# One more seven-product pair in each of five feed-forward stages that also sum modulation vectors, and an earlier split ahead of the gates

## The reference

```python
def swiglu(h, w_gu, w_down):                       # width 1024 -> 2 x 2816 -> 1024
    gate, up = jnp.split(h @ w_gu, 2, axis=-1)
    return (jax.nn.silu(gate) * up) @ w_down

for i in range(DEPTH):                             # 4 layers
    x = x + 0.5 * swiglu(rmsnorm(x, ffn1_norm[i]), ffn1_w_gu[i], ffn1_w_down[i])
    x = x + mixer_i(rmsnorm(x, mix_norm[i]))       # gated delta net, stick-breaking, sparse attention, gated delta net
    x = x + 0.5 * swiglu(rmsnorm(x, ffn2_norm[i]), ffn2_w_gu[i], ffn2_w_down[i])

m = jnp.split((jax.nn.silu(c) @ mod_w[i] + mod_b[i])[:, None, :], N_MOD, axis=-1)      # 9 vectors of 1024 for each of 2 layers
mc = jnp.split(jax.nn.silu(c_ctx) @ mod_w[i] + mod_b[i], N_MOD, axis=-1)               # of these only the first 5 of layer 0
```

## Time and profile before

| | us |
|---|---|
| median of 3 runs | 3553.44 |
| profiled execution | 3552.46 |
| its span | 3550.7 |
| PE busy | 3453.6 (97%) |
| DVE busy | 2463.1 (69%) |
| ACT busy | 1846.2 (52%) |
| POOL busy | 145.2 (4%) |

### The profile page before, as it was taken

How to read it: one execution, slowest core, us unless ns; L and a number is a source line. 1 busy time by engine, 2 the same in 40 slices (tenths; PEclk the granted TensorE clock), 3 DMA queues, 4 the chain that set the end, 5 groups by cost and what they waited for, 6 DMA issues and landing times. The chain is left out here.

```text
span 3550.7 us, 45283 instructions
## 1 busy us (share of the span) xinstructions
PE 3453.6 (97%) x18348; PEld 2924.5 (82%) x18348; DVE 2463.1 (69%) x2749; ACT 1846.2 (52%) x2151; POOL 145.2 (4%) x152
## 2 busy tenths in 40 slices
PE   9999999999999998999999999999999999999999
PEld 7889888888888888788889878787889678788877
DVE  5776657666666678566677668787866567786586
ACT  5454354544645445545454456666654455655464
POOL 0001100000000000000001100000000000000000
PEclk9999999999999999999999999999999999999999
DMA  6642156664467663576752157575744247574574
GB/s 265 239 154 84 60 190 237 220 235 172 157 255 266 255 243 119 202 276 247 272 189 101 67 185 259 201 249 197 245 151 166 72 154 249 196 249 140 189 233 161
DMA packets 95741, 692.40 MB, mean 195 GB/s; under 512 B 10672, under 2 KB 10800, under 8 KB 12208
## 3 DMA queue, kind: packets, MB, share of 16 engines
q1 hardware_dynamic: 79344, 574.15, 43.0%
q0 software_dynamic: 16192, 115.35, 11.5%
HBM read 650.66 MB, written 1.05 MB: 184 GB/s over the span
## 5 line engine op out<-in xcount | busy, mean ns | idle before, releaser
L2392 DVE TENSOR_TENSOR w_lo<-raw,w_hi 128x2048 fp32r<-128x2048 f32 x468 | 1067.6, 2289 | 330.7 <-ACT w_hi L1662 330.5
L1662 ACT ACTIVATE w_hi<-raw 128x2048 fp32r<-128x2048 f32 (+1 forms) x470 | 895.5, 1909 | 372.5 <-PE acc L702 259.5
L700 PE MATMUL wrk<-w_hi,h_hi 128*128 128x512 f32 (+1 forms) x2040 | 796.1, 390 | 13.8 <-issue 5.4
L702 PE MATMUL wrk<-w_hi,h_lo 128*128 128x512 f32 (+1 forms) x2040 | 784.2, 384 | 0.0
L701 PE MATMUL wrk<-w_lo,h_hi 128*128 128x512 f32 (+1 forms) x2040 | 783.0, 384 | 0.0
L700 PEld LDWEIGHTS wrk<-w_hi,h_hi 128*128 128x128 f32 x2040 | 384.3, 188 | 94.5 <-issue 15.8
L700 PE MATMUL acc<-w_hi,hid_hi 128*128 128x512 f32 (+1 forms) x1160 | 453.5, 391 | 4.2 <-DVE hid_lo L2494 3.7
L702 PE MATMUL acc<-w_hi,hid_lo 128*128 128x512 f32 (+1 forms) x1160 | 450.1, 388 | 0.0
L701 PE MATMUL acc<-w_lo,hid_hi 128*128 128x512 f32 (+1 forms) x1160 | 449.7, 388 | 0.0
L702 PEld LDWEIGHTS wrk<-w_hi,h_lo 128*128 128x128 f32 x2040 | 383.9, 188 | 77.0
L701 PEld LDWEIGHTS wrk<-w_lo,h_hi 128*128 128x128 f32 x2040 | 384.6, 189 | 71.2 <-issue 0.2
(11 more groups left out here) (326 smaller groups left out, 4969.2 us busy)
## 6 DMA issues: line engine op xcount, KB each, us to landing
raw<-in_wts SPq DMA_DIRECT2D x469, 1024.0 KB, 4.9
arena<-in_mods POOLq DMA_DIRECT2D x72, 1024.0 KB, 5.1
arena<-in_wts SPq DMA_DIRECT2D x72, 1024.0 KB, 7.7
arena<-arena POOLq DMA_DIRECT2D x36, 1024.0 KB, 7.5
const<-in_const SPq DMA_DIRECT2D x1, 2112.0 KB, 17.3
c<-in_bias POOLq DMA_DIRECT2D x8, 256.0 KB, 2.9
x<-in_x SPq DMA_DIRECT2D x2, 512.0 KB, 6.7
c<-in_c SPq DMA_DIRECT2D x1, 1024.0 KB, 4.9
```

Of the source, the lines that this page charges most:

```text
L700: nc.tensor.matmul(o, l_h, r_h, start=first, stop=False, skip_group_check=True)
L702: return nc.tensor.matmul(o, l_l, r_h, start=False, stop=last, skip_group_check=True)
L1662: return nc.scalar.activation(o, i, f, **kw)
L2392: tt(w_lo[:, ns % SLOTS, :], v, w_hi[:, ns % SLOTS, :].bitcast(F32), ALU.subtract).then_inc(lo_ready, 1)
```

## The change

1. Five stages of the first block (`ffn1_1`, `ffn2_1`, `ffn1_2`, `ffn2_2`, `ffn1_3`), all with modulation, get one pair at step 5. `ffn1_0` and `ffn2_0` stay without.
2. The modulation jobs are single operations of 128 x 1024 on chunks of 512 KB (before: two operations on 1 MB). Their buffers leave the arena: `m_raw` is now `h_tok` (two chunks), `m_prod` is `row`; the last operation on a chunk writes its product over the chunk itself. POOL starts the loads of a stage when the norm's statistics are done (they use `h_tok`), and ACT waits at the start of every feed-forward stage for the jobs before it.
3. In a stage with a pair `mod_plan` shares the jobs over the ten units by `room`: none in unit 0 and in the pair, 3 in unit 1, 2 in the one ahead of the pair, 4 in each other. Up to four are set singly: behind `hid_low`, behind `gated`, and behind each of the two splits that follow. For 26 jobs this gives 0, 2, 4, 3, 2, 0, 4, 3, 4, 4, for the 28 jobs of `ffn1_1` 0, 2, 4, 4, 2, 0, 4, 4, 4, 4. POOL's T3 and T4 additions stand between its chunk loads.
4. In `ffn_pairs` of all stages, a unit that follows a single step splits the piece behind d (the next g(s+1,0), or the first block B11) ahead of the silus (ACT) and ahead of the `gated` operations (DVE). And the sum T2 of a stage's first pair is no longer preceded by the split of B21.

```diff
-PAIRS = {n: (2, 5, 8) for n in ("ffn2_3", "b0_ctx", "b0_ffn0", "b0_ffn1", "b1_ffn0", "b1_ffn1")}
+PAIRS = {n: (5,) for n in ("ffn1_1", "ffn2_1", "ffn1_2", "ffn2_2", "ffn1_3")}
+PAIRS |= {n: (2, 5, 8) for n in ("ffn2_3", "b0_ctx", "b0_ffn0", "b0_ffn1", "b1_ffn0", "b1_ffn1")}
...
-MOD_JOBS = [(m, w) for m in range(MOD_PIECES) for w in range(2 if 2 * m < CTX_CHUNKS else 1)]
+MOD_JOBS = [(k, w) for k in range(2 * MOD_PIECES) for w in range(2 if k < CTX_CHUNKS else 1)]
...
+def mod_plan(name):
+
+    plan, jobs = units(name), mod_jobs(name) if name in MOD_OPS else []
+    pair = [kind == "pair" for kind, _ in plan] + [False]
+    room = [0 if k == 0 or pair[k] else 2 if pair[k + 1] else 3 if k == 1 else 4 for k in range(len(plan))]
+    ends = [len(jobs) * sum(room[:k + 1]) // sum(room) for k in range(len(plan))]
+    return [jobs[a:b] for a, b in zip([0] + ends, ends)]
...
-        m_raw, m_prod = area(3072, 2, PW), area(3072 + 2 * PW, 2, PW)
+        m_raw, m_prod = h_tok, row
... (ScalarE, ffn_pairs)
-                    split_to(at("d", owed[-1]))
+                    split_to(at("d", owed[-1]) + (len(owed) == 1))
... (ScalarE, main loop)
-                if kind in ("gdn", "sb", "dsa") and mods_before(i):
+                if kind in ("gdn", "sb", "dsa", "ffn") and mods_before(i):
... (VectorE, modulation)
-                m, w = MOD_JOBS[g]
-                l = 2 * m // (9 * KC)
-                dve.wait_ge(mod_landed[m % 2], 16 * (m // 2 + 1))
-                if g:
+                k, w = MOD_JOBS[g]
+                l = k // (9 * KC)
+                dve.wait_ge(mod_landed[k % 2], 16 * (k // 2 + 1))
+                v, last = m_raw[:, k % 2, :], g + 1 == len(MOD_JOBS) or MOD_JOBS[g + 1][0] != k
+                if not last and g > 1:
+                    dve.wait_ge(mod_sums, g - 1)
+                elif last and w:
                     dve.wait_ge(mod_sums, g)
-                for b in range(2):
-                    j = 2 * m + b - l * 9 * KC
-                    ins = stt(m_prod[:, b, 0:D], m_raw[:, m % 2, b * D:(b + 1) * D], 1.0, m_rows[:, w, :], ALU.mult, ALU.mult, accum_out=der[:, l, w, j:j + 1])
+                j = k - l * 9 * KC
+                ins = stt(v if last else m_prod[:], v, 1.0, m_rows[:, w, :], ALU.mult, ALU.mult, accum_out=der[:, l, w, j:j + 1])
                 ins.then_inc(mod_sums, 1)
... (VectorE, ffn: of a step's jobs two, not one, stand behind hid_low)
-                    for g in mine[:1]:
+                    for g in mine[:2]:
... (VectorE, ffn_pairs)
                     if ahead is not None:
                         add_blocks("T1", ahead)
+                    mine = jobs[k]
+                    for g in mine[:1]:
+                        modulation(g)
...
-                    split_to(at("d", owed[-1]))
+                    split_to(at("d", owed[-1]) + (len(owed) == 1))
                     gated(s, 0)
                     gated(s, 1)
+                    for g in mine[1:2]:
+                        modulation(g)
                     split_to(at("d", owed[-1]) + 1)
+                    for g in mine[2:3]:
+                        modulation(g)
                     if ahead is not None:
-                        if ahead == PAIRS[name][0]:
-                            split_to(at("d", owed[-1]) + 2)
                         add_blocks("T2", ahead)
                     if s < STEPS - 1:
                         split_to(at("d", owed[-1]) + 2)
+                    for g in mine[3:]:
+                        modulation(g)
                 hid_low(STEPS - 1)
... (GpSimd, modulation)
-                if before(i, "x"):
-                    pool.wait_ge(x_new, before(i, "x"))
+                pool.wait_ge(rstd_ready, 2 * before(i, "norm") + 2)
...
+                for n, mine in enumerate(jobs):
+                    if n + 1 < len(plan) and plan[n + 1][0] == "pair":
+                        block_sum(i, plan[n + 1][1], "T3")
+                    if plan and plan[n][0] == "pair":
+                        block_sum(i, plan[n][1], "T4")
+                    for g in mine:
+                        k, w = MOD_JOBS[g]
+                        if k + 2 < end and (g + 1 == len(MOD_JOBS) or MOD_JOBS[g + 1][0] != k):
+                            pool.wait_ge(mod_sums, g + 1)
+                            load(k + 2)
```

More of the change, by code:

```diff
@@ L125 @@
 CTX_CHUNKS = 5 * KC
[L127 removed]
+MOD_JOBS = [(k, w) for k in range(2 * MOD_PIECES) for w in range(2 if k < CTX_CHUNKS else 1)]
 def mod_jobs(name):
     a = mod_start(name)
[L133 removed]
+    return [g for g, (k, _) in enumerate(MOD_JOBS) if a <= k // 2 < a + MOD_SHARE[name]]
+def mod_plan(name):
[4 more added lines that the diff above has]
+    return [jobs[a:b] for a, b in zip([0] + ends, ends)]
 ARENA = 15104
@@ L2513, in ffn @@
                         split_to(ns + 3 * s + 3)
-                    for g in mine[1:]:
+                    for g in mine[2:]:
                         modulation(g)
@@ L2627, in ffn_pairs @@
                     dve.wait_ge(rstd_ready, 2 * before(i, "norm") + 2)
+                jobs = mod_plan(name)
                 factors()
@@ L3393, in gdn, with block_sum @@
                                                 ALU.mult).then_inc(stage("gdn_lts"), 1)
+            def block_sum(i, s, which):
+                g = starts[i]["pairs"] + PAIRS[ops[i][1]].index(s)
+                if which == "T3":
+                    pool.wait_ge(block_landed[HOME["B22"]], 16 * (g + 1))
+                    pool.wait_ge(sum_ready, 2 * g + 1)
+                else:
+                    pool.wait_ge(lo_ready, ring_at[i, ("B21", s)] + 1)
+                    pool.wait_ge(sum_ready, 2 * g + 2)
+                pool.dma_start(blocks[HOME[which]], blocks[HOME[ADDED[which]]], accum_op=ALU.add).then_inc(added[which], 16)
@@ L3395, in modulation @@
             def modulation(i, name):
-                start = mod_start(name)
                 if name in ROWS_IN:
                     pool.wait_ge(taken, use[name, "mrow3"] + 1)
-                if before(i, "x"):
-                    pool.wait_ge(x_new, before(i, "x"))
[L3403 to L3413, removed]
+                pool.wait_ge(rstd_ready, 2 * before(i, "norm") + 2)
+                end = 2 * (mod_start(name) + MOD_SHARE[name])
+                def load(k):
+                    v = mods_d[k // 2]
+                    pool.dma_start(m_raw[:, k % 2, :], v[:, k % 2 * D:(k % 2 + 1) * D]).then_inc(mod_landed[k % 2], 16)
@@ new lines, in modulation @@
+                load(2 * mod_start(name))
+                load(2 * mod_start(name) + 1)
+                plan = units(name) if name in PAIRS else []
+                jobs = mod_plan(name) if plan else [mod_jobs(name)]
+                for n, mine in enumerate(jobs):
[8 more added lines that the diff above has]
+                            load(k + 2)
@@ L3433, in attn @@
                         load(n + 1)
[L3435 to L3448, removed]
             pool.wait_ge(ident_loaded, 16)
@@ L3460, in _ @@
                     modulation(i, name)
-                if name in PAIRS:
-                    block_sums(i, name)
+                elif name in PAIRS:
+                    for s in PAIRS[name]:
+                        block_sum(i, s, "T3")
+                        block_sum(i, s, "T4")
 def chunks(v):
```

## The result

The changed kernel takes 3562.74 us (median of 13 runs, 3556.97 to 3574.64) against 3553.78 us of the kernel before (13 runs, 3549.52 to 3556.31); the ratio is 1.0027, interval 1.0019 to 1.0035. It is slower by 9 us, forecast were 3.5 us less. Its profiled execution took 3559.18 us (span 3557.3), 6.7 more than that of before.

A forecast was written before the change was run, and what follows sets the result against it. It took PE, busy for 97% of the span, as the bound. Terms -17.7 - 11.5 + 5.5 + 15.1 + 5.1 = -3.5 us against 3552.46 us gave 3549 us, own range 3543 to 3556.

The forecast's parts named there:

- Part 1: Six stages that already had pairs: the new order removes the first pair's gap and its clock drops, -17.7 us.
- Rival (d): First pairs of the old pair stages: reordering does nothing, since B21 takes T2's place; +17.7, 3567 us; chance 0.06.
- Part 2: Five new pairs: -11.5 us from fewer matmuls, +5.5 us from their openings, entries at nothing.
- Rival (b): Entry to the new pairs is late behind two jobs; up to 18 us, 3558 to 3567 us; chance 0.13.
- Part 3: Last step of the five stages: jobs and a late chunk, landing in 3.7 us, delay `hid_low(10)`; +15.1 us.
- Part 4: Clock at the new gaps in the five stages: 3.9 drops of 1.3 us, +5.1 us.
- at 5.1 us 5.6 more: Last step, bound over four stages: if a 512 KB load lands in 5.1 us, 5.6 us more loss.
- (a): Last step: the last chunk isn't late enough to matter; 3539 us, or 3543 with two drops; chance 0.27.
- (c): Last step: the last chunk lands as late as the slowest load, 8.2 us; +18, 3567 us; chance 0.06.

The follow-up runs named there:

- the order alone: The kernel before with only the earlier split and the sum T2 ahead of B21's split in the six old pair stages; 3535.5 us, ratio 0.9951.
- low_first: The changed kernel with hid_low(10) ahead of the third and fourth modulation job in the last unit; 3550.75 us, ratio 0.9995.
- last_one: The changed kernel with one modulation job instead of four in the last unit of the five stages (two in `ffn1_1`); 3541.03 us, ratio 0.9966.
- no_new_pairs: The changed kernel without its five new pairs, keeping 512 KB chunks, their buffers and the new order; 3535.0 us, ratio 0.9951.

## Why the prediction was wrong

**Part 1, right.** Forecast -17.7, measured -18.7 in the changed kernel and in the order alone. The gap is gone in all six stages, no drop follows, and `ffn2_3` is 184.4 us where 184.6 was forecast. Rival (d) is out.

**Part 2, nearly right.** Pairs and openings by themselves bring -5.8, forecast was -6.0. The five openings lose 1.1 us each, as forecast. The entries were put at nothing, with 0.1 us of room; they lose 1.0, 0.8 and 1.0 us in three of the four stages with one job on a chunk, 2.9 us in all. Rival (b) looked for this at the second job of the entry and set it aside, since "that chunk is asked for some 10 us ahead". For that job this holds: it was 11.0 us in `ffn2_1`, and the load took 8.6. The wait is at the last job of the unit before, whose chunk is asked for 4.4 us ahead of its turn and takes 9.4 us (in `ffn1_2` and `ffn1_3` 9.5 and 9.4; in `ffn2_2` the same job waits 4.2 us and PE loses nothing). The units with several jobs were priced by the jobs' own durations, 13.0 us of 16.8, without any wait for a chunk; with the wait `hid_low` starts 2.0 us behind the transposes (1023.92 to 1025.93) and not 1.26, more than the 0.1 us of room.

**Part 3, the step that failed.** "I take 3.7" us for the landing of 512 KB. The last loads of the four stages took 5.1 to 5.6 us, and the ones before them 4.9 to 8.0. PE's end gaps are 2.4, 3.8, 6.6, 4.3 and 6.5 us (start to start less 0.227), 23.7 together, against 18.0 forecast in part 4: 5.7 us more. The bound "at 5.1 us 5.6 more" is just that. The mechanism was right, each gap ends on `hid_lo` behind chunk waits, and `ffn1_1` came out near the 2.2 us of the forecast. Wrong was to price a half-size load by its size, between a 256 KB load and 1 MB loads: the median landing was 5.5 us against 5.1 for the whole piece. Sorted by what the program had in flight at the issue, the 144 loads say more. Seven had nothing beside them and took 4.0 to 4.4 us, still more than 3.7. With one weight load in flight (77) the median is 4.9, from 3.9 to 9.8; with a weight load and another chunk (26) it is 6.1. The 1 MB loads of before had 5.1 in both of the first two cases. The last loads of the four stages were issued 3.1 us behind a weight load. Why a half-size load gains so little beside others stays open. Rivals (a) and (c) are out: no load took less than 3.9 us, and the last ones were far from 8.2.

The Trainium skill ("DMA: Bandwidth & Descriptors", "Anatomy of one DMA") would give 3.2 us, an estimate by its fixed cost and rate. No load of a chunk in any trace here took less than 3.8 us, and the medians were 5.2 to 6.0 where all 144 are loaded; the measurement decides.

**Part 4, too small.** Forecast 3.9 drops of 1.3 us, 5.1 us; there were five, behind every end gap, of 1.4 to 1.6 us each. Behind them 33 matmuls are spaced 0.43 us instead of 0.227, and with the partly slow ones beside them that is 7.6 us: 2.5 more. Even the gap of 2.4 us had its drop. The three drops of before, counted in the same way, cost 1.4 us each; the 1.3 came from counting whole matmuls in stretches of 3.4 us.

**The sum.** 5.7 at the end gaps, 2.9 of entries and 2.5 of clock are 11.1 of the 11.8 us by which the five stages miss the forecast. The rest, 0.7 us, I have not placed. The profiled execution is 6.7 us over that of before, and the median of the runs another 2 us more. The runs of the changed kernel spread over 17.7 us, those of `low_first` over 16.3, those with three buffers over 2.9 to 7.2; but those are 5 runs each where the first two have 13 and 11, and `last_one` waits as much and spreads over 4.3 in 6. What makes that spread stays open.

Seen by the runs, the whole is a gain of 18 us by the order and a loss of 27 us by the five pairs as they are fed here.

## What to carry to other kernels

When work that reads streamed chunks is bunched, take the chunk's landing from the slowest loads in the busiest stretch of the trace, not from its size, and count how many jobs ahead it is asked for: a third buffer was worth 25 us in the five stages here (30 us between the medians), without any load landing sooner. Moving such a job, or what stands behind it, only moves the wait as long as the chunk is late (`last_one`, `low_first`); once it is there, order works. A gap of 2 us or more in front of PE is to be priced with a likely drop of the clock, 1.4 to 1.6 us here.

## What the runs showed of the hardware

Loads of 512 KB issued by POOL landed in 5.2 us (median) in `no_new_pairs`, where no block loads run in these stages, in 5.3 to 6.0 us and up to 14.4 in the kernels with the five pairs, though the loads of 1 MB before the change had 5.1. With nothing of the program in flight at their issue they took 4.0 to 4.4 us in the changed kernel. Of PE's end gaps of 2.2 to 2.4 us in the changed kernel and the one with three buffers, three of four were followed by 8 matmuls at half clock (granted clock 0.50), and all four of the longer ones by 5 to 8. It is not so everywhere: in `last_one` PE waits 3.7 us at the entries of both `ffn2_1` and `ffn1_3`, and only the second is followed by a drop. Small products on constants, 0.219 us each, in the end gaps kept the granted clock of the stages at 1.00.
